# Three loads of the expert stream, each cut into pieces of 112, 8 and 8 partitions

## The reference, cut to what matters

```
def run_block(args):
    toks, wts, e = args
    xb = hf[toks]
    y = (jax.nn.silu(xb @ w_gate[e]) * (xb @ w_up[e])) @ w_down[e]
    return y * wts[:, None].astype(y.dtype)
```

## Time and profile before

| | |
|---|---|
| median of three runs | 1600.22 us (1599.81 to 1601.59) |
| the profiled execution, its own time | 1601.27 us |
| its span in the trace | 1599.2 us |
| granted TensorE clock, mean | 0.997 |
| PE busy | 98% |
| DMA, mean over the span | 234 GB/s; in the part of the experts about 425 GB/s |
| HBM read | 372.28 MB |

### The profile page before, as it was taken

How to read it: one execution, slowest core, us unless ns; L and a number is a source line. 1 busy time by engine, 2 the same in 40 slices (tenths; PEclk the granted TensorE clock), 3 DMA queues, 4 the chain that set the end, 5 groups by cost and what they waited for, 6 DMA issues and landing times.

```text
span 1599.2 us, 20633 instructions
## 1 busy us (share of the span) xinstructions
PE 1571.1 (98%) x8775; PEld 1000.2 (63%) x8775; DVE 895.9 (56%) x1549; ACT 192.5 (12%) x311; POOL 36.1 (2%) x60
## 2 busy tenths in 40 slices
PE   8999999999999999999999999999999999999997
PEld 4866499974458564999744976899543333333332
DVE  5896766764659876676646676785432213221122
ACT  1321000000114110000001331410000000000001
POOL 1001000000010010000000000000000000000000
PEclk9999999999999999999999999999999999999999
DMA  6532545563634326355427333456999999999997
GB/s 211 206 106 105 179 146 164 169 216 105 212 105 159 106 105 217 113 173 185 170 105 255 113 106 132 158 182 265 375 413 425 427 425 429 424 425 427 428 421 284
DMA packets 129780, 374.68 MB, mean 234 GB/s; under 512 B 17220, under 2 KB 65672, under 8 KB 116888
## 3 DMA queue, kind: packets, MB, share of 16 engines
q1 hardware_dynamic: 118864, 370.62, 61.0%
q10 hardware_dynamic: 10824, 2.72, 0.7%
HBM read 372.28 MB, written 1.05 MB: 233 GB/s over the span
## 4 chain that ended last, share of the span: by engine, by line
PE 89%; DMA 8%; DVE 2%; SPq 1%; issue 0%; ACT 0%; POOL 0%; POOLq 0%; DVEq 0%
PE bank L870 16%; PE bank L1182 16%; PE bank L801 10%; PE bank L1619 10%; PE bank L813 6%; PE bank L1665 6%; PE bank L1435 4%; DMA turned_rows<-in_w_down 3%; PE bank L1385 3%; DMA h<-in_w_down 3%; DMA weights<-in_w_down 2%; PE bank L1307 2%; PE bank L1165 2%; PE bank L1468 2%; PE bank L1317 2%; PE bank L821 2%
## 5 line engine op out<-in xcount | busy, mean ns | idle before, releaser
L801 PE MATMUL bank<-weights,turned_rows 128*128 128x512 f32 x384 | 169.7, 599 | 0.4 <-DVE turned_rows L2109 0.4
L3256 DVE TENSOR_TENSOR bc<-mix,bank 128x512 f32<-128x512 f32 x16 | 17.2, 1076 | 217.2 <-PE bank L1619 217.2
L870 PE MATMUL bank<-arena 128*128 128x512 f32 x296 | 133.2, 592 | 0.0
L801 PEld LDWEIGHTS bank<-weights,turned_rows 128*128 128x128 f32 x384 | 72.7, 192 | 86.6 <-issue 85.6
L1182 PE MATMUL bank<-arena 128*128 128x128 f32 x960 | 110.5, 275 | 0.0
L1182 PEld LDWEIGHTS bank<-arena 128*128 128x128 f32 x960 | 108.8, 192 | 0.0
L870 PEld LDWEIGHTS bank<-arena 128*128 128x128 f32 x296 | 56.0, 190 | 69.9 <-issue 67.9
L813 PE MATMUL bank<-turned_rows,weights 128*128 128x256 f32 x448 | 98.6, 380 | 0.0
L813 PEld LDWEIGHTS bank<-turned_rows,weights 128*128 128x128 f32 x448 | 84.6, 190 | 12.1 <-issue 0.7
L1619 PE MATMUL bank<-arena,rows_late 128*64 128x512 f32 x248 | 88.8, 595 | 0.8 <-DMA weights<-in_w_up 0.7
L1665 PE MATMUL bank<-arena,mix 128*32 128x512 f32 x480 | 79.4, 595 | 3.0 <-DMA turned_rows<-in_w_down 2.2
(11 more groups left out here) (538 smaller groups left out, 2557.2 us busy)
## 6 DMA issues: line engine op xcount, KB each, us to landing
weights<-in_w_in SPq DMA_DIRECT2D x28, 2048.0 KB, 8.0
arena<-in_w_gate SPq DMA_DIRECT2D x13, 2048.0 KB, 23.7
arena<-in_w_up SPq DMA_DIRECT2D x12, 2048.0 KB, 35.4
weights<-in_w_ffn_gate SPq DMA_DIRECT2D x22, 1024.0 KB, 5.4
weights<-in_w_ffn_up SPq DMA_DIRECT2D x22, 1024.0 KB, 8.1
weights<-in_w_ffn_down SPq DMA_DIRECT2D x10, 2048.0 KB, 7.9
arena<-in_w_down SPq DMA_DIRECT2D x10, 2048.0 KB, 30.8
weights<-in_w_up SPq DMA_DIRECT2D x9, 2048.0 KB, 20.6
```

The costliest lines, as they stand in the source:

```text
L801: ins = mm(b[:, :], xT[:, k, t0 + P * t:t0 + P * t + P], w[:, k, :], start=(k == 0), stop=(k == KD - 1))
L870: ins = mm(b[:, :], lhs[:, j, :], rhs[:, j, :], start=(first and j == 0), stop=(last and j == pairs - 1))
```

## The change

Loads 23, 45 and 67 of the stream, all three of slot 1, are no longer one transfer of 128 partitions. Each is issued as three transfers: partitions 0 to 111, partitions 112 to 119, and partitions 120 to 127, each with the whole 16 KB of a partition. The bytes, their places, the slot, the semaphore and the wait ahead of the load stay as they were. The count in `landed_at` goes from one transfer to three for these loads.

```
+LEANED = (23, 45, 67)
...
+            elif i in LEANED:
+                parts = 3
             elif i >= len(LOAD_ORDER) - 4:
                 parts = 0
             landings[i % NXS] += parts
...
                 if i % NXS == SPLIT:
                     split_load(i, split_slot)
+                elif i in LEANED:
+                    for r, rows in ((0, 112), (112, 8), (120, 8)):
+                        sp.dma_start(expert_slot[i % NXS][r:r + rows, :], wsrc[c6][2 * n + c6 % 2][r:r + rows, :]).then_inc(sem(f"expert_chunk{i % NXS}"), 16)
                 else:
                     expert_load(i % NXS, c6, n)
```

## The result

The changed kernel takes 1626.47 us (median of five runs, 1625.98 to 1627.66), the kernel before, in five runs taken beside them, 1600.59 (1599.81 to 1601.59). The ratio is 1.0163, 95% interval [1.0151, 1.0174]: slower by 25.9 us. The forecast was 1611.4 with a range up to 1620. The sign and the place were right; the size was not.

A forecast was written before the change was run, and what follows sets the result against it. DMA bounds the kernel: load 87's landing on the slowest engine plus a fixed tail. Per load 0.62 + 3.70 + 0.62 = 4.94 us; 14.8 over three, less a 3.6 lead, adds 11.2: 1611.4 us, range 1598.4 to 1620.

The forecast's parts named there:

- What bounds the kernel: In the experts, load 87, the chain's last DMA, landing on the slowest engine sets the end, plus a fixed tail.
- Issue on SP at nothing: Six more issues on SP at 0.43 us, 2.6 us in all, cost nothing because the engines' queues are never empty.
- Small pieces, 3.70 us per load: Two transfers of 8 partitions per changed load, four partitions after each other, 1.85 us excess each.
- The 112 piece, 0.62 us per load: In each changed load, engines writing partitions 0 to 111 may meet another engine's writes; one partition's time, 0.62 us, was taken.
- its upper bound of 4.3 us: For the 112-partition transfer: each of an engine's seven partitions meets another, 7 x 0.617 = 4.3 us per load.
- an excess of 0.3 and of 0.8 us per small piece: Small-piece costs at which, on the front half, the end stays put (0.3) or moves 3.2 us later (0.8).
- One half pays, with a lead of 3.6 us to use up: Eight engines carry nine partitions, losing 14.8 us over three loads; if the front half, its 3.6 us lead comes off.
- the plateau at 213: At the stream's end, half the full rate in GB/s, eight engines still working; forecast to stay or get longer.
- All after one another: Rival: each small piece's eight partitions go serially, 4.94 us; 29.6 us over three loads less 3.6, 1626 us; chance 0.05.
- Even halves: Rival: small pieces move side by side on the front half, 112 piece free; gain 1.2 us, 1599.0 us; chance 0.26.
- the earlier entry of the chain into DMA: Sign of the forecast: in the experts, the chain of waits goes into DMA earlier than 1388 us.
- the landing near 1557: Sign of the forecast: load 87, late in the experts, lands near 1557 us instead of 1545.51.

The follow-up runs named there:

- e1: Kernel before with loads 23, 45 and 67 each cut by columns into three transfers of all 128 partitions (3584, 256, 256 columns): 1601.18 us.
- e2: Kernel before with loads 23, 45 and 67 each as two transfers, 112 and 16 partitions: 1621.36 us, ratio 1.013.
- e4: Kernel before with only load 45 cut into 112, 8 and 8 partitions: 1608.4 us, ratio 1.0049.
- e13: Kernel before with only load 45 cut, into partitions 32 to 95, then 0 to 31, then 96 to 127: 1603.8 us, ratio 1.0023.
- e3: Kernel before with loads 23, 45 and 67 each as two transfers of 64 neighbouring partitions (0 to 63, 64 to 127): 1622.76 us, ratio 1.0149.
- e9: Kernel before with loads 23, 45 and 67 each as the 64 even partitions, then the 64 odd ones: 1600.98 us, ratio 1.0002.

## Why the prediction was wrong

**What bounds the kernel: right.** The end moved with the landing of load 87: +26.9 us there, +25.2 at the last down stage, +25.9 in the time. The tail behind the landing was 1.7 us shorter, so it isn't quite as fixed as the prediction had it.

**Issue on SP at nothing: right in the cost, wrong in the size.** The prediction took 0.43 us for each issue from the earlier trace rows, which show load 23 only; the three issues of load 67 took 2.4 to 4.8 us each. e1 has the same number of transfers, with issues as long, and costs nothing.

**Small pieces, 3.70 us per load: about right, as far as the runs tell.** No run has them alone. One piece of 16 in their place (e2) takes 25.9 - 20.6 = 5.3 us away, 1.8 per load, but that piece lies in the same corner and costs something itself. The second part of the hole of e4 puts them at some 3 us.

**The 112 piece, 0.62 us per load: this is the step that failed.** With the 16 that complete it, it costs 6.9 us per load (e2); the first part of the hole of e4 puts the piece itself at 4 to 5 us, and e13 beside e4 shows that the rate falls as soon as it is in front. The prediction named the mechanism, an engine that writes where another writes, and its upper bound of 4.3 us, and then took the low end because the earlier trace rows show no meeting in the present shape. That was the wrong reason: the rows show what 128 partitions do, and the question was about another shape. The bound, seven partitions that each wait once for one other, is near what it cost. The two values that the prediction gives for no change and for a loss of 3.2 us, an excess of 0.3 and of 0.8 us per small piece, have the 112 piece at nothing, not even at the 0.62 of its own sum; with 0.62 they would be 0 and 0.5. They make the small pieces the question, where the 112 piece was.

**One half pays, with a lead of 3.6 us to use up: failed.** The sum was made for the eight engines with nine partitions. The holes go down to 156 GB/s, below the 213 of a half at work, so the engines of both halves lose. (That an engine which is met in its lane is slowed like the one that comes to it would explain this; no run shows single engines.) So no lead was taken off, and none was left at the end: the plateau at 213, which the prediction expected to stay or grow, has gone. One load alone cost its whole hole (e4).

In the sum: 3 x 4.94 - 3.6 = 11.2 us was forecast. Measured are 6.1 + 8.9 + 9.2 = 24.2 us in the holes. With the upper bound of 4.32 for the 112 piece in place of 0.62, and no lead taken off, the prediction's own sum is 3 x (0.62 + 3.70 + 4.32) = 25.9 us. That it meets the measured 25.9 so closely is in part luck, since the loads cost 6.1 to 9.2 us in the holes, and a load alone 7.6.

**The rivals.** "All after one another" gave 1626, the measured time, but by another way: 4.32 us for each piece of 8 and 0.62 for the 112 piece, less the lead. The two small pieces of e4 lose some 3 us and not 8.6, so this rival wasn't the cause either, and its number was met by luck. "Even halves" needed the 112 piece to be free, which e4 beside e13 refutes. Of what was to show the forecast, the dips behind the three loads and the earlier entry of the chain into DMA came, the landing near 1557 and the plateau didn't.

The sentence of the Trainium skill that the prediction quoted on ports ("SBUF — State Buffer", section "Door 1: The DMA port swizzle") was applied to the pieces of 8 only. The half rate of e3 and the full rate of e9 agree with applying it to large pieces too, by the ports that they reach. The 112 partitions reach all 16 ports by it and were slow all the same: how many ports a transfer reaches doesn't price it alone.

## What to carry to other kernels

In a stream that already saturates the DMA engines, keep every load at all 128 partitions, and where it has to be cut, cut by columns, or into 64 or 32 partitions that lie two or four apart; both cost nothing here, where the cuts of a 2 MB load into blocks of neighbours cost 3.0 to 14.5 us. Before pricing an unusual shape from even rows, ask whether those rows contain that shape at all. A busy share of 1.0 doesn't say that bytes flow: read the GB/s beside it.

## What the runs showed of the hardware

- A busy DMA engine need not move bytes at its rate. In the holes the share stays at about 1.00 with 187 to 275 GB/s; the same share carries 426 outside.
- Which partitions (with their rows in HBM) go together decides, not how many: 64 even ones 420 to 428 GB/s, 64 neighbours from 0 or 64 on 205 and 213, and 434 in the two us in which partitions 32 to 95 stand in front.
- Where the matrix engine ran dry behind a hole its clock followed. Load 45's and load 67's holes in the changed kernel, in stretches of 10 us: busy 5.91 us in one, and then the granted clock at 0.50, that is 1.2 GHz of 2.4, in the next.

```profile
1340.00:1350.00 10.00, 5.91 (x28) 1.72 (x24) 1.03 (x1) 0.00 (x0) 0.00 (x0) 0.99 1.01 202
1350.00:1360.00 10.00, 5.50 (x28) 1.59 (x32) 0.00 (x0) 0.00 (x0) 0.00 (x0) 0.50 0.97 351
...
1460.00:1470.00 10.00, 6.34 (x30) 2.03 (x26) 0.00 (x0) 0.60 (x1) 0.00 (x0) 0.96 1.00 226
1470.00:1480.00 10.00, 5.32 (x14) 1.80 (x16) 0.00 (x0) 0.00 (x0) 0.00 (x0) 0.53 0.98 375
```

That the slower clock cost little here is argued: the engine waited for loads in those stretches, and 24.2 of the 25.9 us are in the holes.
